# First stage of a one-core hybrid layer: the norm's weights as one row spread by TensorE, and a seven-bank ring for the turned tiles

## The reference

```python
def rms_norm(x, g):
    y = x * lax.rsqrt(jnp.mean(x * x, axis=-1, keepdims=True) + RMS_EPS)
    return y * g

h = rms_norm(x, norm_g)                       # x: 1024 x 2048, norm_g: 2048
proj = jnp.einsum('bsd,de->bse', h, w_in)     # 14 groups of columns
# A: 12 heads of dilated window attention, B: 8 heads of forgetting attention,
# C: 4 heads of gated linear attention, each gated by silu of its own columns
return x + jnp.einsum('bse,ed->bsd', mixed, w_out)
```

## Time and profile before

| | |
|---|---|
| time, median of 3 runs | 2057.22 us (2056.49 to 2057.32) |
| span of the profiled execution | 2055.0 us |
| TensorE busy (matmul) | 2023.8 us, 98% |
| VectorE busy | 1021.3 us, 50% |
| ScalarE busy | 859.1 us, 42% |
| GpSimd busy | 398.2 us, 19% |
| granted TensorE clock | 1.000 |

### The profile page before, as it was taken

One profiled execution on the slowest core, in us unless ns is written; L12 is line 12 of the kernel. 1 busy time (PEld: TensorE's weight loads), 2 busy tenths in 40 slices (PEclk: granted clock), 3 DMA queues, 4 the chain that ended last, 5 costly groups with the idle time before them and its releaser, 6 DMA issues.

```text
span 2055.0 us, 28736 instructions
## 1 busy us (share of the span) xinstructions
PE 2023.8 (98%) x10108; PEld 1705.1 (83%) x10108; DVE 1021.3 (50%) x1629; ACT 859.1 (42%) x1448; POOL 398.2 (19%) x330
## 2 busy tenths in 40 slices
PE   6999999999999999999999999999999999999999
PEld 5788888888888888888888888888888888788887
DVE  6711356465545555555555555555555568512122
ACT  7311344444454445455454445455444456311110
POOL 0000343251521222122221222122221210000000
PEclk9999999999999999999999999999999999999999
DMA  7322423433332222222222222322232283323134
GB/s 234 79 72 71 114 68 108 109 82 105 82 98 77 71 79 78 87 66 85 68 77 87 73 76 88 98 67 89 85 97 87 67 289 127 127 88 129 51 128 153
DMA packets 192457, 201.10 MB, mean 98 GB/s; under 512 B 15992, under 2 KB 141992, under 8 KB 191232
## 3 DMA queue, kind: packets, MB, share of 16 engines
q1 hardware_dynamic: 175664, 169.70, 28.3%
q10 hardware_dynamic: 16720, 30.45, 4.0%
HBM read 151.33 MB, written 48.78 MB: 97 GB/s over the span
## 4 chain that ended last, share of the span: by engine, by line
PE 89%; DVE 4%; ACT 2%; DMA 2%; issue 1%; POOL 1%; SPq 0%; DVEq 0%; ACTq 0%; POOLq 0%
PE acc L1953 19%; PE acc L1955 19%; PE acc L1954 19%; PE pv L2192 4%; PE turned L2177 4%; PE scores L2169 2%; PE scores L2166 2%; PE scores L2282 1%; PE scores L2283 1%; PE turned L2282 1%; PE acc L2283 1%; PE acc L2282 1%; PE turned L2283 1%; PE acc L2284 1%; PE turned L2284 1%
## 5 line engine op out<-in xcount | busy, mean ns | idle before, releaser
L1953 PE MATMUL acc<-act_hi,w_hi 128*128 128x512 f32 x1848 | 737.0, 399 | 1.1 <-DVE w_lo L1446 0.7
L1955 PE MATMUL acc<-act_hi,w_lo 128*128 128x512 f32 x1848 | 722.0, 391 | 0.0
L1954 PE MATMUL acc<-act_lo,w_hi 128*128 128x512 f32 x1848 | 720.7, 390 | 0.0
L1955 PEld LDWEIGHTS acc<-act_hi,w_lo 128*128 128x128 f32 x1848 | 346.8, 188 | 75.7
L1953 PEld LDWEIGHTS acc<-act_hi,w_hi 128*128 128x128 f32 x1848 | 347.4, 188 | 67.9 <-DVE w_lo L1446 3.7
L1954 PEld LDWEIGHTS acc<-act_lo,w_hi 128*128 128x128 f32 x1848 | 347.6, 188 | 65.0
L1446 DVE TENSOR_TENSOR w_lo<-w_raw,w_hi 128x512 fp32r<-128x512 f32 x223 | 199.4, 894 | 357.8 <-ACT w_hi L997 357.5
L1303 ACT ACTIVATE prob<-prob,neg_max 128x128 f32<-128x128 f32 (+7 forms) x160 | 124.0, 775 | 250.9 <-DVE neg_max L1757 250.9
L997 ACT ACTIVATE w_hi<-w_raw 128x512 fp32r<-128x512 f32 x223 | 139.1, 624 | 136.4 <-PE acc L1955 110.0
L1773 DVE TENSOR_TENSOR pt_lo<-turned,pt_hi 128x1024 fp32r<-128x1024 f32 (+1 forms) x120 | 114.9, 957 | 145.6 <-ACT pt_hi L1311 144.9
L1311 ACT ACTIVATE pt_hi<-turned 128x1024 fp32r<-128x1024 f32 (+1 forms) x120 | 97.6, 814 | 200.0 <-PE turned L2177 199.6
(11 more groups left out here) (337 smaller groups left out, 2897.7 us busy)
## 6 DMA issues: line engine op xcount, KB each, us to landing
w_raw<-in_w_in_dram SPq DMA_DIRECT2D x240, 256.0 KB, 2.9
proj_scratch<-stage ACTq DMA_DIRECT2D x116, 256.0 KB, 2.1
w_raw<-in_w_out_dram SPq DMA_DIRECT2D x71, 256.0 KB, 3.2
raw<-proj_scratch SPq DMA_DIRECT2D x20, 512.0 KB, 3.4
act_lo<-mixed_scratch SPq DMA_DIRECT2D x7, 1024.0 KB, 7.4
res<-in_x_dram SPq DMA_DIRECT2D x24, 256.0 KB, 5.7
out_dram<-res SPq DMA_DIRECT2D x24, 256.0 KB, 2.8
extra_raw<-in_w_out_dram SPq DMA_DIRECT2D x23, 256.0 KB, 3.5
```

Of the source, the lines that this page charges most:

```text
L1953: pe.matmul(acc, hi, xh, start=first, stop=False)
L1954: pe.matmul(acc, hi, xl, start=False, stop=False)
L1955: mm = pe.matmul(acc, lo, xh, start=False, stop=end)
```

## The change

1. The norm's weights come as two halves of one row on one partition (`g_rows`: a row of `stage` and a row of `c_sum`), by two DMAs of 4 KB on ACT's queue, ahead of its table load. GpSimd writes a row of 128 ones. TensorE multiplies the ones with the row, four float32 matmuls of 512 columns with a contraction of one, into four banks, and DVE copies these into `g_wide`. `normalize(0)` waits for the fourth copy, and so does TensorE's first transpose. The DMA that read the row 128 times is gone from SP's queue.
2. The turned banks of tiles 0 to 3 go round a ring of seven (`turn_place`), with `scores` and the second `acc` bank beside the four; a bank waits for the one that used its place before (`turn_before`). Tiles 4 to 7 use the old four.
3. TensorE turns tile 3 between first parts (0, 0) and (1, 0), not behind both. On ACT `turned_hi(2)` stands ahead of the split of the second quarter, and `row_scale(4)` ahead of `turned_hi(3)`. On DVE `turned_lo(2)` stands ahead of the split of the second quarter.

```diff
+TURN_PLACES = 7
+def turn_place(t, b):
+    return (4 * t + b) % TURN_PLACES if t < NT // 2 else b
+def turn_before(t, b):
+    places = [(u, c) for u in range(t + 1) for c in range(4) if (u, c) < (t, b) and turn_place(u, c) == turn_place(t, b)]
+    return 4 * places[-1][0] + places[-1][1] + 1 if places else None
-        turn_banks = [turned[:, 0:HALF], turned[:, HALF:], pv[:], side[:]]
+        turn_banks = [turned[:, 0:HALF], turned[:, HALF:], pv[:], side[:], scores[:, 0:HALF], scores[:, HALF:], bank[1][:]]
+        g_rows = [stage[0:1, :, :].rearrange("p a b -> p (a b)"), c_sum[0:1, :]]
+        ones_row = small[0:1, 0:P]
@@ sync
             load_x(0)
-            sp.dma_start(g_wide[:], norm_g[0:1, :].broadcast_to([P, D_MODEL])).then_inc(g_in, 16)
             for t in range(1, X_BUFS):
@@ gpsimd
             pool.memset(eps_col[:], EPS).then_inc(eps_ready, 1)
+            pool.memset(ones_row, 1.0).then_inc(eps_ready, 1)
@@ scalar
+            for h in range(2):
+                act.dma_start(g_rows[h], norm_g[0:1, h * SEQ:(h + 1) * SEQ]).then_inc(g_in, 16)
...
             row_scale(3)
+            turned_hi(2)
             split_hi_half(0, 1)
-            turned_hi(2)
+            row_scale(4)
             turned_hi(3)
-            row_scale(4)
@@ vector
                 if t == 0:
-                    dve.wait_ge(g_in, 16)
+                    for b in range(4):
+                        dve.wait_ge(g_in, 33 + b)
+                        dve.tensor_copy(g_wide[:, b * HALF:(b + 1) * HALF], banks[2 + b]).then_inc(dist_chain, 1)
+                    dve.wait_ge(dist_chain, 4)
...
             normalize(3)
+            turned_lo(2)
             split_lo_half(0, 1)
-            turned_lo(2)
             turned_lo(3)
@@ tensor
                 for b in range(4):
-                    if t >= 1:
-                        pe.wait_ge(x_lo_done, 4 * (t - 1) + b + 1)
+                    if turn_before(t, b) is not None:
+                        pe.wait_ge(x_lo_done, turn_before(t, b))
...
+            pe.wait_ge(eps_ready, 2)
+            pe.wait_ge(g_in, 32)
+            for b in range(4):
+                pe.matmul(banks[2 + b], ones_row, g_rows[b // 2][:, (b % 2) * HALF:(b % 2 + 1) * HALF], start=True,
+                          stop=True).then_inc(g_in, 1)
+            pe.wait_ge(dist_chain, 4)
             pe.wait_ge(consts, 8)
             for t in range(3):
                 turn_tokens(t)
-            for kq in range(2):
-                first_part(kq, 0)
+            first_part(0, 0)
             turn_tokens(3)
+            first_part(1, 0)
```

More of the change, by code:

```diff
@@ L1082, in turned_hi @@
                     act.activation(act_hi[:, 4 * b:4 * b + 4, t * P:(t + 1) * P],
-                                   turn_banks[b].rearrange("p (k t) -> p k t", k=4), ACT.Copy).then_inc(x_hi_done, 1)
+                                   turn_banks[turn_place(t, b)].rearrange("p (k t) -> p k t", k=4), ACT.Copy).then_inc(x_hi_done, 1)
             def evac_half(n):
@@ L1476, in turned_lo @@
                     at = (slice(None), slice(4 * b, 4 * b + 4), slice(t * P, (t + 1) * P))
-                    dve.tensor_tensor(act_lo[at], turn_banks[b].rearrange("p (k t) -> p k t", k=4),
+                    dve.tensor_tensor(act_lo[at], turn_banks[turn_place(t, b)].rearrange("p (k t) -> p k t", k=4),
                                       act_hi[at].bitcast(F32), ALU.subtract).then_inc(x_lo_done, 1)
@@ L1508, in _ @@
             split_lo_half(2, 1)
-            step = [0]
+            step = [4]
             def link(ins):
@@ L1987, in turn_tokens @@
                 for b in range(4):
-                    if t >= 1:
-                        pe.wait_ge(x_lo_done, 4 * (t - 1) + b + 1)
+                    if turn_before(t, b) is not None:
+                        pe.wait_ge(x_lo_done, turn_before(t, b))
                     for k in range(4):
                         f = 4 * b + k
-                        mm = pe.transpose(turn_banks[b][:, k * P:(k + 1) * P], x_buf[t % X_BUFS][:, f * P:(f + 1) * P],
+                        mm = pe.transpose(turn_banks[turn_place(t, b)][:, k * P:(k + 1) * P], x_buf[t % X_BUFS][:, f * P:(f + 1) * P],
                                           ident[:])
```

## The result

The changed kernel takes 2060.16 us (median of 20 runs, 2059.18 to 2062.96), the kernel before 2056.93 (20 runs, 2055.23 to 2059.51): a ratio of 1.0016, with a 95% interval of 1.001 to 1.0022. It is slower by 3.2 us. That is inside the 0.2% which the prediction called no change, but outside its range of 2054.8 to 2060.0, and 3.1 above its forecast of 2057.1. The profiled span went from 2055.0 to 2058.1.

The account below looks back on a forecast made before the run. TensorE is busy 98%, so only early idle counts: loads, then the ACT, DVE and TensorE loop, then tile 4. Late start +1.3, pauses -1.0, tile 4 -0.5, new wait 0.5: sum 0.0, put -0.1, 2057.1; range 2054.8 to 2060.0.

Parts of the forecast that it names:

- The rows are there at 4.0: Start of kernel: the two 4 KB row loads on ACT's queue land at 4.0 us, ends 3.2 and 5.9.
- The third rival: Row loads land late beside tile 0's load: +1.8 to +3.3, or +3.1 to +5.8 if later still; chance 0.10.
- Four matmuls take 7.0 and end the pause at +0.8: Row matmuls at the low clock take 7.0 us, to 11.0; DVE's copies end at 11.8, where `normalize(0)` starts.
- The upper level from tile 0 on: TensorE at 2.4 GHz from tile 0's transposes: 0.44 a bank, `row_scale(2)` at 16.8, 1.5 us later than before.
- the second rival: Clock stays low through tiles 0 and 1, or falls back in the pause before them: +0.6 to +1.5; chance 0.23.
- From `normalize(2)` to the last low part 12.3, without a pause: DVE, tiles 2 to 3: from 19.4 to 31.7 in 12.3 us, before 13.3; 1.0 of pauses goes.
- tile 4 is ready then: Behind tile 3's first parts: tile 4 turned from 35.4 against 35.95, -0.5; the pause of 0.59 goes.
- the wait of 0.5 before half job (0, 3): Behind tile 5's squares and normalize: the weights' fourth quarter is ready at 40.4, half job (0, 2) ends at 39.9.
- The sum: Whole early chain of tiles 0 to 5: 0.0 with rounding, put at -0.1 us; chance 0.35 within half a microsecond.
- The first rival: Clock rises inside the four row matmuls: -1.0 to -1.8, at best -2.2; 2055.4 to 2056.2; chance 0.27.
- the 2.4 us which the change could bring: Without the 1 MB `g_wide` load tile 1 lands at 8.3, so DVE may start it at 11.0, not 13.44.
- Behind it TensorE is full as before: Behind the new wait at half job (0, 3): TensorE has no further pauses, so early shifts carry to the end.

Follow-up runs that it names:

- the kernel kept busy: Fastest version (split fast row, tile 2's and 3's squares sooner) plus unused TensorE work in its pauses: three float32 products, 24, 18 and 10 transposes; 2057.0 us, ratio 1.0001.
- the better placed one: Fastest version plus unused transposes only: 17 straight behind the row's matmuls, 18 before tile 2's last bank, 10 before first part (0, 0); 2055.63 us, ratio 0.9992.
- the fastest kernel: Changed kernel with the row in one load, eight one-pass fp32r matmuls on its high and low parts, and squares and normalizes of tiles 2 and 3 sooner; 2054.22 us.

## Why the prediction came out wrong

By its own steps, in order.

**The rows are there at 4.0: failed.** They were there at 5.5, near the end of 5.9 that was kept for the range. The third rival named this mechanism, two small loads beside 4 MB, and priced it at +1.8, or +3.3 with the low level behind it as well; +3.2 came. I gave it a chance of 0.10 on the argument that nothing makes a queue wait for another's megabyte. The runs say otherwise: with the rows first, both are there at 2.74; with one load of 8 KB on ACT's queue, at 3.77; with two of 4 KB there, at 5.51. The first row moved between 1.7 and 1.8, just ahead of tile 0's packets, the second between 4.8 and 4.9, when these were nearly through; on which of the 16 engines it stood is not shown. The Trainium skill (DMA: Bandwidth & Descriptors, "Queues, rings and completion order") has each DMA engine take turns between queues, a packet at a time, and a packet there is a run of many descriptors. Tile 0's megabyte is 128 pieces of 8 KB in this trace, eight for each of 16 engines on average. A second row that moves 3.1 us after the first, with tile 0 nearly through, agrees with that rule if such a run of eight is one packet; no run here shows that.

**Four matmuls take 7.0 and end the pause at +0.8: right.** 1.71 each (1.74 was worked out from a matmul of 192 columns), 7.0 together, and `normalize(0)` 0.9 behind them. The conversion by columns held, and that one row costs as much as 128 too (4.63 for five matmuls of 256 columns, over one row as over 128).

**The upper level from tile 0 on: failed.** This step rested on the sentence that the first run is as long as both of before together. It counted time at work. Tile 0 was at the lower level and so was the start of tile 1; `row_scale(2)` stands 4.2 behind the first transposes (15.93 to 20.11), not 2.5. That is the 1.6 of the second rival, on top of the third. The two kernels with a warm-up show what was wrong with it: matmuls over one row kept TensorE busy for 11.5 us without a change of level; with a warm-up over 128 rows the level rose, and it fell again at 9.8, as the one-row matmuls ended and ahead of the 3.26 of idle time. Of the second rival's two halves, a clock that stays low and one that falls back in the pause, the change shows the first: its level first rises in tile 1.

**From `normalize(2)` to the last low part 12.3, without a pause: right.** 22.69 to 35.0. The step "tile 4 is ready then" and the wait of 0.5 before half job (0, 3) are right as well: tile 4 to tile 5 takes 7.75, before 7.29, a new 0.46. The ring and the order alone gave -1.7 where this part of the sum has -1.0 for the pauses and -0.6 at tile 4.

**The sum.** -0.1, plus 1.6 for the late rows (13.43 for 11.8), plus 1.7 for tile 0 at the lower level (4.2 for 2.5): +3.2. Two terms were mis-sized, and both of them stood in the text as rivals. The third rival's +3.3 even had both in it, but that rival had a chance of 0.10 in all, and the range took only its earlier half. (The first rival's prices don't follow from the chain either: `normalize(0)` at 9.3 in place of 11.8 would give -2.6 by it, and -1.8 is written without a term that stops it.)

**The loads, "the 2.4 us which the change could bring": failed, and it was no term of the sum.** Tile 1's squares do start at 8.39, as forecast. But with the row early and fast, nothing came of it. The chain from tile 0's normalize over its transposes and ACT's high parts to `row_scale(2)` holds in any case, and the order of ACT's own queue decides. With another order 0.7 more came by the medians (2054.22 for 2054.91), which is within the noise.

**"Behind it TensorE is full as before": right for the change, not for every start.** For the change the shift at tile 5 (3.28) is the shift at the end (3.1). But a lead is not kept as surely as a lag. Against the kernel before, tile 4 was turned 3.0 us sooner in the kernel kept busy, 4.1 in its second execution and 3.9 in the better placed one; at the end of the span they stood 0.7 behind it, 0.7 behind it and 0.7 ahead. The waits at 238 and near 1686, and the lower level behind three of them, took most of what was lost.

## What to carry to other kernels

A small load that others wait for belongs ahead of the large ones (shown on SP's queue), and where it can't be, one load is better than two: its own size says nothing of when it comes. To replace a load by TensorE's work at the start of a kernel, price that work at the lower clock level, and what runs behind it too; here neither the length of that work nor its end in a pause told the level. And before a load is made smaller, look for what stands ahead of the next step in its engine's queue: here that was ACT's order, not the data.

## What was not expected of the hardware

- TensorE busy from 1.32 to 12.8 us with float32 matmuls over one row stayed at the 1.2 GHz level throughout (1.71 for 512 columns); five of the same over 128 rows brought the 2.4 GHz level for the matmuls behind them (two in 1.88 at 8.01, against 3.62), and it was gone at 9.8, after 3.8 us of one-row matmuls.
- Transposes raise the level as well. In the kernel before nothing else had run ahead of 21.19, where the upper level shows; in the fastest kernel, after 3.77 us of idle time, tile 0's banks begin at 11.54 with 1.94 for two, and its fourth, at 14.12, takes 0.67. The Trainium skill (TensorE: Matmul & The Clock Gate, "Part 4: PE-mode transpose") says that they do not count as other matmuls do; here they did.
- Behind pauses of 1.82, 1.92 and 2.26 us (at 238.04, 1685.92 and 1687.44) the level was the lower one; after 1.58, 1.75 and 1.80 it stayed, and in the changed kernel even after 3.55, in front of tile 2 at 25.10 (four transposes in 0.66). With the ring alone, a bank behind a pause of 2.69 was still at the upper level (0.65 at 20.53) and the third one behind it at the lower (1.06 at 21.47). The pause's length alone doesn't settle it.
- Until the level first changes, the granted clock of the stretches reads 1.00 although the records are twice as long (0.85 for a bank in tile 0 of the changed kernel); there the records' own lengths have to be read. Behind the first change it follows the level: 0.50 through tile 0 of the full-row warm-up.
- The same kernel in two executions can start at different levels: the kernel kept busy had its split row's first two records in 1.22 and in 0.80.
- Two loads of 4 KB on one queue, asked for 0.6 us apart, moved 3.1 us apart beside a tile's load; ahead of it both are there at 2.74.
